# One hundred and twelve unread matrix products behind the last scatter of a two-layer decoder trunk

## The reference

```python
for i in range(DEPTH):                                   # DEPTH = 2
    h = rms_norm(x, attn_norm[i])
    proj = jnp.einsum('bsd,de->bse', h, w_in[i])
    sb = stick_breaking_attention(...)                   # 8 heads of 64
    df = differential_attention(...)                     # 4 heads of 128
    x = x + jnp.einsum('bse,ed->bsd', jnp.concatenate([sb, df], axis=-1), w_out[i])
    h2 = rms_norm(x, ffn_norm[i])
    x = x + (swiglu(h2, ...) if i % 2 == 0 else moe_swiglu(h2, router_w[j], ...))
return rms_norm(x, final_norm)
```

## Time and profile before

| | us |
|---|---|
| median of two executions | 1404.01 (1403.14 to 1404.88) |
| span of the profiled execution, first to last instruction | 1401.0 |
| PE busy | 1386.3 (99%) |
| PEld busy | 1180.9 (84%) |
| DVE busy | 1139.5 (81%) |
| ACT busy | 934.6 (67%) |
| last TensorE product starts | 1391.53 |

### The profile page before, as it was taken

How to read it: one execution, slowest core, us unless ns; L and a number is a source line. 1 busy time by engine, 2 the same in 40 slices (tenths; PEclk the granted TensorE clock), 3 DMA queues, 4 the chain that set the end, 5 groups by cost and what they waited for, 6 DMA issues and landing times.

```text
span 1401.0 us, 19232 instructions
## 1 busy us (share of the span) xinstructions
PE 1386.3 (99%) x7369; PEld 1180.9 (84%) x7369; DVE 1139.5 (81%) x862; ACT 934.6 (67%) x751; POOL 37.4 (3%) x53
## 2 busy tenths in 40 slices
PE   9999999999999999999999999999999999999997
PEld 8888999889888888888888888888888888888885
DVE  6866565556857999888988888898888889889897
ACT  5555443445555877777777777777777777777775
POOL 0010000000010020000000000000000000001100
PEclk9999999999999999999999999999999999999999
DMA  9734985556424999999999999999999999999992
GB/s 336 265 114 147 393 326 187 191 170 199 155 98 163 356 389 393 396 394 397 371 395 390 361 387 392 374 371 389 394 350 396 391 361 383 393 378 364 396 395 114
DMA packets 191039, 448.80 MB, mean 320 GB/s; under 512 B 8515, under 2 KB 11274, under 8 KB 190986
## 3 DMA queue, kind: packets, MB, share of 16 engines
q1 hardware_dynamic: 189162, 441.74, 85.9%
q0 software_dynamic: 1616, 5.77, 1.0%
q10 hardware_dynamic: 208, 0.54, 0.1%
HBM read 429.67 MB, written 18.36 MB: 320 GB/s over the span
## 4 chain that ended last, share of the span: by engine, by line
PE 97%; DVE 1%; DMA 1%; ACT 1%; SPq 1%; issue 0%; DVEq 0%; ACTq 0%
PE ps L550 90%; PE ps L1009 2%; DMA raw<-in_w_in 1%; PE ps L681 1%; PE ps L712 0%; PE ps L968 0%; PE ps L735 0%; PE ps L670 0%; PE ps L639 0%; ACT w_hi L380 0%; PE ps L700 0%; PE ps L695 0%; PE ps L701 0%; PE ps L682 0%; PE ps L623 0%; PE ps L724 0%
## 5 line engine op out<-in xcount | busy, mean ns | idle before, releaser
L385 DVE TENSOR_TENSOR w_lo<-raw,w_hi 128x2048 fp32r<-128x2048 f32 x401 | 915.0, 2291 | 187.2 <-ACT w_hi L380 186.4
L380 ACT ACTIVATE w_hi<-raw 128x2048 fp32r<-128x2048 f32 x400 | 766.5, 1918 | 295.7 <-PE ps L550 286.7
L550 PE MATMUL ps<-w_hi,xe_hi 128*128 128x512 f32 x896 | 244.7, 395 | 0.6 <-DVE xe_lo L1846 0.6
L550 PE MATMUL ps<-w_hi,xe_lo 128*128 128x512 f32 x896 | 240.0, 390 | 0.0
L550 PE MATMUL ps<-w_lo,xe_hi 128*128 128x512 f32 x896 | 239.9, 389 | 0.0
L550 PEld LDWEIGHTS ps<-w_hi,xe_lo 128*128 128x128 f32 x896 | 168.2, 188 | 35.8
L550 PEld LDWEIGHTS ps<-w_lo,xe_hi 128*128 128x128 f32 x896 | 168.2, 188 | 35.4
L550 PEld LDWEIGHTS ps<-w_hi,xe_hi 128*128 128x128 f32 x896 | 164.6, 188 | 32.4 <-issue 0.8
L550 PE MATMUL ps<-w_hi,he_hi 128*128 128x512 f32 x448 | 120.9, 391 | 0.0
L550 PE MATMUL ps<-w_lo,he_hi 128*128 128x512 f32 x448 | 120.3, 390 | 0.0
L550 PE MATMUL ps<-w_hi,he_lo 128*128 128x512 f32 x448 | 120.1, 389 | 0.0
(11 more groups left out here) (250 smaller groups left out, 960.9 us busy)
## 6 DMA issues: line engine op xcount, KB each, us to landing
raw<-in_expert_w_gate SPq DMA_DIRECT2D x112, 1024.0 KB, 7.4
raw<-in_expert_w_up SPq DMA_DIRECT2D x112, 1024.0 KB, 7.5
raw<-in_expert_w_down SPq DMA_DIRECT2D x112, 1024.0 KB, 7.4
raw<-in_w_in SPq DMA_DIRECT2D x23, 1024.0 KB, 6.2
raw<-in_dense_w_gate SPq DMA_DIRECT2D x11, 1024.0 KB, 7.1
raw<-in_dense_w_up SPq DMA_DIRECT2D x11, 1024.0 KB, 7.6
raw<-in_dense_w_down SPq DMA_DIRECT2D x11, 1024.0 KB, 5.0
raw<-in_w_out SPq DMA_DIRECT2D x8, 1024.0 KB, 5.7
```

What stands on the lines that cost most here:

```text
L380: nc.scalar.activation(half_of(w_hi, n), raw[:, n % RAW, :], ACT.Copy).then_inc(hi_ready, 1)
L385: nc.vector.tensor_tensor(half_of(w_lo, n), raw[:, n % RAW, :], half_of(w_hi, n).bitcast(F32), ALU.subtract).then_inc(lo_ready, 1)
L550: return pe.matmul(o, stationary, moving, start=start, stop=stop, skip_group_check=True)
```

## The change

The change adds a helper `unread` and 28 calls of it, all after the two loops of `scatter` in TensorE's program. Each call issues four products into PSUM bank 2 (`ps[:, 2, ...]`), each with `start=True` and `stop=True`; none waits for a semaphore and none signals one. With `back=True` the output's columns are written from the last to the first.

```diff
                 for t in range(TT):
                     scatter(t, o)
+            def unread(moving, stationary, times=4, back=False):
+                n = moving.shape[1]
+                for i in range(times):
+                    o = ps[:, 2, n - 1::-1] if back else ps[:, 2, 0:n]
+                    pe.matmul(o, stationary, moving, start=True, stop=True, skip_group_check=True)
+            def columns(begin, n=CH):
+                return w_hi[:, 0, P // 8 + begin:P // 8 + begin + n]
+            def backwards(begin, n=CH):
+                return w_hi[:, 0, P // 8 + begin + n - 1:P // 8 + begin - 1:-1]
+            rows = xe_hi[:, 0, :]
+            two = xe_hi[:, 0:2, :].rearrange("p k n -> p (k n)")
+            unread(columns(0), rows)
+            unread(columns(0), xe_hi[:, 0, 0:1].to_broadcast([P, P]))
+            for begin in (16, 0, 32, 48, 64, 80, 96, 112):
+                unread(backwards(begin), rows, back=True)
+            unread(backwards(32), rows)
+            for begin in (4, 8, 16, 24, 32, 48, 64, 80, 96, 112):
+                unread(columns(begin), rows)
+            unread(two, columns(0, P))
+            unread(two, columns(32, P))
+            unread(xe_hi[:, 0:2, :].rearrange("p k n -> p (k n)")[:, ::-1], columns(0, P), back=True)
+            unread(xe_hi[:, 0:2, :].rearrange("p k n -> p (k n)")[:, ::-1], columns(32, P), back=True)
+            unread(two, columns(0, 1).to_broadcast([P, P]))
+            unread(columns(0, 1).to_broadcast([P, CH]), rows)
+            unread(columns(0, 1).to_broadcast([P, CH]), xe_hi[:, 0, 0:1].to_broadcast([P, P]))
```

## The result

The changed kernel takes 1418.12 us (median of two executions, 1418.01 to 1418.24) against 1404.01 before: a ratio of 1.0103, 95% interval 1.0084 to 1.0122. The forecast was 1418.4 us. The profiled execution has a span of 1416.0 us (before: 1401.0).

What follows compares the result with a forecast made beforehand. The tail was taken to bound the added work: 23.2 us of products less 9.0 us of cover, plus 0.2 of drain. 1401.0 + 14.4 + 3.0 = 1418.4 us; range 1415.0 to 1430.0, 8 times in 10.

Steps and rivals of the forecast that it cites:

- The cover: In the tail, 9.0 us from TensorE's next possible product to SP's drain, in which unread products would cost nothing.
- The start: Behind the last scatter, the first added product could start at 1391.53 + 0.23 = 1391.76 us.
- The stream: TensorE's 112 added products: 92 x 0.2274 + 20 x 0.113 us, 23.2 us in all, every form at the contiguous rate.
- no difference between the first four, the backward ones and the shifted ones: Sign in the profile after: starts of the 84 products 0.227 us apart throughout, whatever their form.
- The term of the 256-wide ones: 20 added products with 256 moving columns at 0.113 us each, 2.26 us.
- The end: At the block's end, TensorE drains last, at 1415.1 us, and the span ends at about 1415.4.
- The term of 3.0 us around the span: Time outside the profiled span, left at 3.0 us: the median 1404.01 against the span of 1401.0.
- The rate: Price of a 512-wide product, start to start in the earlier trace: 0.2274 us, preferred to the skill's 215.8 ns.
- Half rate for backward outputs: Rival at the PSUM writes: backward outputs cost twice the price, adding 8.2 us, 1426.6 us; chance 0.12.
- stepped reads: Rival: all moving patterns with a step other than one run at half rate, adding 10.9 us, 1429.3 us; chance 0.08.
- The steep factor for backward products: Rival: backward products cost more than 2.7 times the price, slower by over 2%; at four times 1443.0 us; chance 0.06.
- The clock rival: Rival: TensorE's clock falls to its lower level under the added products, doubling all 23.2 us to 1441.6 us; chance 0.04.

Runs made afterwards that it cites:

- run with 36 products: Changed kernel with only the first 36 of its 112 products kept; 1403.6 us beside 1404.04 for the kernel before, ratio 0.9999.
- run ahead of the scatters: Changed kernel with all 112 products issued ahead of the scatters instead of behind them; 1426.62 us, ratio 1.0163.

## Why the prediction was right

**The cover.** 9.0 us were forecast; in the trace after it is 9.1, from 1391.93 to SP's drain at 1401.0. The run with 36 products fits 8.4 us of work into it at no cost, and the run ahead of the scatters shows the bill without it, 22.6 us by the median against 14.1. Shown.

**The start.** 1391.76 was forecast and 1391.93 measured; the last scatter itself stood 0.16 us later in this execution.

**The stream.** 92 x 0.2274 + 20 x 0.113 = 23.2 us were forecast and 23.6 measured (from 1391.93 to 0.22 us behind the last start, at 1415.34). The parts, as means over the starts in the trace: the first four 0.231, with a repeated stationary column 0.232, backwards with a backward output 0.234, backwards with a forward one 0.2335, from shifted places 0.231, 256 wide 0.119, moving column repeated 0.218. The sign "no difference between the first four, the backward ones and the shifted ones" was wrong in detail. The 84 products were all dearer than 0.2274, the groups by 1.5 to 3%, which added 0.4 us, and the eight with the repeated column were 4% cheaper, which gave back less than 0.1. The stream felt 0.4 of 23 us, because no form was far off. The term of the 256-wide ones was too low by 5% (0.119 for 0.113), 0.1 us; blocks of plain ones stood at 0.120 too, so this is not the backward reading. Why the 15 products of the earlier trace rows stand at 0.113 and these do not stays open.

**The end.** 1415.4 was forecast for the span's end, 1416.0 measured: 0.45 us from the stream, 0.17 from the start. The term of 3.0 us around the span hid the difference. It was a median less the span of one execution. The profiled execution after took 1418.24 us with a span of 1416.0, so 2.2 us lie outside, and in the executions of the other runs it is 2.2 to 2.4 us (1.8 in one). The 3.0 was thus some 0.7 too high, probably because the profiled execution of before was a shorter one than the median, and this made up for the 0.6 by which the span's end was forecast too low. Such differences are ordinary: 15 executions of the kernel before, beside the run with 36, have spans from 1400.1 to 1402.6 us. So the agreement to 0.3 us is luck. Inside the traces, the added time is 14.8 us where 14.4 was forecast; that agreement, and the mechanism behind it, are not luck.

**The rate.** The estimate by the Trainium skill ("TensorE: Matmul & The Clock Gate", section Back-to-back issue gap), 215.8 ns for 512 columns, was set aside for the row's 227. The runs show both: 215.7 for bfloat16 and for columns read four times each, 226.7 for reduced float32 read contiguously. Since the data made no difference there (zeros and ones stood at 0.2265 us), the 5% come from how the moving operand is read. The prediction took the formula as one for a stream, as Part 1 of that page does. The section itself calls it the gap of an isolated product and gives about 131 ns for 512 columns in a stream of loads and products; no run here shows that, for no block of 512-wide products settles below 215 ns each.

**The rivals.** Half rate for backward outputs (0.12) and for stepped reads (0.08) did not come about at a step of minus one, but both exist at other steps, at the price that was put on them: for reads a step of two in reduced float32, for outputs a step of two in bfloat16. The steep factor for backward products (0.06) falls with their 0.234 us. The clock rival (0.04) was refuted for these products, while a starved stream does meet it.

## What to carry to other kernels

Before costing work that is added at the end of an engine's program, look for who is last at the meeting point: here the first 9 us of a 99% busy engine were free, and ahead of the same few instructions they cost everything. Take the price of a product from start to start in a stream of the same format and width, and expect reversed, repeated or shifted operands to move it by a few per cent only; a step of two in a reduced float32 moving operand, or in the output of a bfloat16 product, doubles it. Take the time outside the span from one execution's own time and span, and leave a microsecond or two for what executions differ by.

## What was not expected of the hardware

- Contiguous reduced float32 as moving operand is slower than bfloat16: 226.7 ns for 512 columns with weights, zeros or ones, against 215.7 for bfloat16 or for columns repeated four times. For the products of this format, most of this kernel, that is an estimated 5% of their time (11.0 of 226.7 ns), which instruction counts don't show.
- A moving step of 8 bytes costs double (452 ns), whether in reduced float32 or bfloat16; 16 bytes cost 460 ns in the one and 900 in the other. In reduced float32, 256 columns that stand 32 bytes apart cost 218 ns, no more for a column than at 16.
- A TensorE that is busy without a gap can lose its clock: under products of 512 columns that took 900 ns each it fell to the lower level within four microseconds, under products that took 460 ns it did not.
